# The first tile's queries ahead of the second's, the gate projection by weight blocks, and another split of the same SBUF between two rings

## The reference, cut to what matters

```
u = rmsnorm(h, mix_norm); proj = u @ w_in          # q,k,v of A; z,x,B,C,dt; q,k,v of C
h += concat(y_a, y_b * silu(z) normed, y_c) @ w_out
u = rmsnorm(h, ffn_norm)
q = (u @ w_query).reshape(b, s, 8, 2, 128)         # 8 heads, 2 halves each
sc = einsum("bshtd,htkd->bshtk", q, sub_keys)      # 128 scores in each half
best 16 of 128 per half, best 16 of the 16 x 16 sums -> idx, gates = softmax
act = gelu(u . expert_u[idx]) * gates              # 128 rows of U per token
h += sum(act * expert_v[idx])                      # 128 rows of V per token
h += sigmoid(rmsnorm(h) @ w_gate) * (p @ w_proj)
```

## Time and profile before

| | |
|---|---|
| median of three executions | 3315.85 us (3302.12 to 3317.89) |
| the profiled execution | 3308.7 us, its span 3307.0 us |
| PE, DVE, POOL, ACT busy | 72%, 66%, 59%, 26% |
| bytes moved by DMA | 1267.10 MB, of which 1073.87 MB are gathers |
| granted TensorE clock, mean | 0.834 of full speed |

### The profile page before, as it was taken

The page is one execution under the profiler, slowest core; times in us unless marked ns, Lnnn a source line. Parts: engine busy times, 40 slices in busy tenths (PEclk is TensorE's granted clock), DMA queues, the critical chain, the costliest instruction groups (busy, mean ns, idle before and its releaser), DMA issues.

```text
span 3307.0 us, 34117 instructions
## 1 busy us (share of the span) xinstructions
PE 2395.4 (72%) x11010; PEld 1176.1 (36%) x11010; DVE 2177.6 (66%) x5271; ACT 861.7 (26%) x2201; POOL 1966.3 (59%) x2064
## 2 busy tenths in 40 slices
PE   8999787877788879768668778668765445555546
PEld 4754445532333546333323445333321111111111
DVE  1344878777656788695666777695657777777750
ACT  2441333342132233340222223331211111111100
POOL 0001556566566667676566666676667777777763
PEclk9999888887899887878889887978887767777668
DMA  5426999999999999999999999999999999999996
GB/s 190 144 96 223 374 400 420 362 399 401 420 421 421 414 420 417 413 393 420 421 420 421 416 419 392 417 404 421 421 420 419 419 420 419 419 420 419 420 416 238
DMA packets 332296, 1267.10 MB, mean 383 GB/s; under 512 B 37288, under 2 KB 43600, under 8 KB 313432
## 3 DMA queue, kind: packets, MB, share of 16 engines
q0 software_dynamic: 294912, 1073.87, 80.4%
q1 hardware_dynamic: 37208, 191.04, 14.5%
HBM read 1256.22 MB, written 12.09 MB: 384 GB/s over the span
## 4 chain that ended last, share of the span: by engine, by line
DMA 33%; PE 26%; POOL 15%; DVE 15%; issue 8%; ACT 3%; POOLq 0%; DVEq 0%; SPq 0%; ACTq 0%
DMA v_ring<-peer_v,idx_v 14%; DMA u_ring<-peer_u,idx_u 13%; POOL v_ring L935 7%; DVE u_ring L1733 7%; PE ps L2195 6%; POOL u_ring L921 6%; PE ps L1924 5%; PE ps L2128 3%; PE ps L2117 3%; DMA front<-peer_v,idx_v 3%; PE ps L2043 2%; DMA front<-peer_u,idx_u 2%; PE ps L2011 1%; POOL front L921 1%; POOL front L935 1%
## 5 line engine op out<-in xcount | busy, mean ns | idle before, releaser
L1733 DVE CUSTOM_DVE_ANT_0 u_ring<-u_ring,ps 128x1024 f32<-128x1024 f32 x917 | 1104.2, 1218 | 486.6 <-DMA u_ring<-peer_u,idx_u 479.1
L921 POOL DMA_INDIRECT u_ring<-peer_u,idx_u x917 | 877.7, 957 | 708.0 <-DVE idx_u L1705 304.0
L935 POOL DMA_INDIRECT v_ring<-peer_v,idx_v x920 | 883.6, 960 | 523.5 <-PE ps L2195 280.0
L2195 PE MATMUL ps<-v_ring,spread 128*32 128x512 f32 x3680 | 690.1, 814 | 568.6 <-DMA v_ring<-peer_v,idx_v 470.2
L1924 PE MATMUL ps<-front 128*128 128x512 f32 x1024 | 455.3, 600 | 3.0 <-ACT front L1216 3.0
L2195 PEld LDWEIGHTS ps<-v_ring,spread 128*32 128x32 f32 x3680 | 138.0, 132 | 881.1 <-issue 879.3
L1924 PEld LDWEIGHTS ps<-front 128*128 128x128 f32 x1024 | 193.1, 192 | 257.8 <-issue 257.5
L2195 PE MATMUL ps<-front,spread 128*32 128x512 f32 x416 | 146.3, 959 | 137.3 <-DMA v_ring<-peer_v,idx_v 104.0
L2128 PE MATMUL ps<-front 128*128 128x512 f32 x512 | 229.9, 606 | 0.4 <-DVE front L1630 0.4
L2043 PE MATMUL ps<-front 128*128 128x256 f32 x768 | 184.9, 396 | 0.5 <-DVE a_neg L1488 0.5
L1733 DVE CUSTOM_DVE_ANT_0 front<-front,ps 128x1024 f32<-128x1024 f32 x107 | 129.9, 1220 | 79.7 <-DMA front<-peer_u,idx_u 78.7
(11 more groups left out here) (266 smaller groups left out, 3045.0 us busy)
## 6 DMA issues: line engine op xcount, KB each, us to landing
front<-weight_blocks SPq DMA_DIRECT2D x140, 1024.0 KB, 7.7
v_ring<-peer_v,idx_v POOLq DMA_INDIRECT x920, 13.5
u_ring<-peer_u,idx_u POOLq DMA_INDIRECT x917, 13.6
front<-x SPq DMA_DIRECT2D x14, 512.0 KB, 8.0
front<-c_bias_all SPq DMA_DIRECT2D x32, 192.0 KB, 5.8
front<-keys_turned SPq DMA_DIRECT2D x4, 1024.0 KB, 12.3
front<-ple_w_gate SPq DMA_DIRECT2D x1, 4096.0 KB, 23.6
out<-front SPq DMA_DIRECT2D x7, 512.0 KB, 6.5
```

Source lines behind the costliest of these rows:

```text
L921: nc.gpsimd.indirect_dma_start(row, None, io["peer_u"][0], bass.IndirectOffsetOnAxis(ap=k.idx_u[:, t % 2, j:j + 1], axis=0)).then_inc(here ...
L935: nc.gpsimd.indirect_dma_start(row, None, io["peer_v"][0], bass.IndirectOffsetOnAxis(ap=k.idx_v[:, m % 2, column:column + 1], axis=0)).the ...
L1733: nc.vector.tensor_tensor_reduce(out=row, in0=row, in1=k.un_ps, scale=1.0, scalar=0.0, op0=ALU.mult, op1=ALU.add, accum_out=k.dots[:, t % ...
L2195: last = mm(k.acc_ps[32 * j:32 * j + 32, half * 512:(half + 1) * 512], centres[:, at:at + 32], row[:, half * 512:(half + 1) * 512], start= ...
```

## The change

Four things change together.

1. The ring of weights has RW = 4 places of half a block (512 KB), 2 MB in place of 3 MB; each block is loaded and given back in two parts (SUB = 2). The SBUF that this frees (2048 columns) goes to two more places for V: RV = 11, and MORE_V falls from 4 to 2, so that the grown ring has 13 places as before. V's gathers begin at slot 33 and not 35.
2. `z` becomes `zh`: one step for each block and both tiles, so each block ends with its own step.
3. In group 0 the first tile goes ahead: its turned activations (`n2_t`) stand before the norm of tile 1, and its `q0` product (`p1`) and its scores before those of tile 1. The other units keep their steps for both tiles.
4. The gates of head 1 (`g_norm` 1) move from before slot 0 to slot 1.

```diff
@@ -38,11 +38,12 @@
 GT = 2
 GROUPS = TILES // GT
 NG = GT * P
-RW, UNIT, WCH = 3, 512, 4
-RU, RV, Q = 7, 9, 4
+RW, UNIT, WCH, SUB = 4, 512, 4, 2
+WR = RW * SUB * UNIT
+RU, RV, Q = 7, 11, 4
 STEPS = P // Q
-MORE_U, MORE_V = 4, 4
+MORE_U, MORE_V = 4, 2
 KEPT = 2
 GROW_U, GROW_V = 735, 693
 EDGE = 4
...
-    c, z, o = c_steps(g), [("z", t, u) for u in range(2) for t in tiles_of(g)], o_steps(g)
+    c, o = c_steps(g), o_steps(g)
+    z = [("zh", g, u, half) for u in range(2) for half in range(2)]
...
-        out += turned[0] + o[2:4] + turned[1] + o[4:] + [("n2", 0, 1), ("n2", 1, 1)]
+        out += turned[0] + o[2:4] + turned[1] + o[4:] + [("n2", 0, 1)]
...
-    return out + [("n2_t", t, half) for t in tiles_of(g) for half in range(2)] + [("hold", g * GT)] * (g > 0)
+    if g == 0:
+        return out
+    return out + [("n2_t", t, half) for t in tiles_of(g) for half in range(2)] + [("hold", g * GT)]
+def first_queries():
+    turned, product = ([[(kind, t, half) for half in range(2)] for t in tiles_of(0)] for kind in ("n2_t", "p1"))
+    keyed = [[("q_t", t, 0), ("q_s", t, 0)] for t in tiles_of(0)]
+    return turned[0] + [("n2", 1, 1)] + product[0] + turned[1] + keyed[0] + product[1] + keyed[1]
...
+    if n == 1:
+        out.append(("g_norm", 1))
...
-    return (front_steps(0) + query_steps(0, [0]) + [] + tops[0] + query_steps(0, [1])
-            + [("un", 0)] + tops[1] + [("g_norm", 0), ("g_norm", 1)])
+    return (front_steps(0) + first_queries() + tops[0] + query_steps(0, [1])
+            + [("un", 0)] + tops[1] + [("g_norm", 0)])
...
-                self.block_end.setdefault(step, []).append(g * UNITS + i)
+                for sub in range(SUB):
+                    self.block_end.setdefault(step, []).append((g * UNITS + i) * SUB + sub)
+                    bank = ended_bank(step) if sub == SUB - 1 else None
+                    freed += bank is None
+                    self.given_back.append((bank, freed))
...
-    def load_block(u):
-        if u >= RW:
-            end = next(step for step, blocks in k.block_end.items() if u - RW in blocks)
-            if end in k.half_no:
-                sp.wait_ge(k.w_free, k.half_no[end] + 1)
-            elif end[0] in ("p", "o"):
-                filled((*end[:3], GT - 1))
+    def load_block(n):
+        if n >= RW:
+            bank, freed = k.given_back[n - RW]
+            if bank:
+                filled(bank)
             else:
-                filled(end)
-        sp.dma_start(k.block(u), k.block_src(u)).then_inc(k.w_in[u % RW], 16)
+                sp.wait_ge(k.w_free, freed)
+        sp.dma_start(k.block(n), k.block_src(n)).then_inc(k.w_in[n % RW], 16)
...
+    def products(g, at, half, keys, tiles, gives=True):
+        for sub in range(SUB):
+            w = block(g, at + half, sub)
+            for key, t in zip(keys, tiles):
+                ps, filled = again(key) if half or sub else open_(key)
+                for j in range(SUB):
+                    c = half * WCH + sub * SUB + j
+                    last = mm(ps, k.uT[:, c, cols(t)], w[:, j, :], start=(c == 0), stop=(c == DCH - 1))
+                if half and sub:
+                    last.then_inc(filled, 1)
+            if gives and not (half and sub):
+                last.then_inc(k.w_free, 1)
...
+    def first_query(t, half):
         if half == 0:
-            last.then_inc(k.w_free, 1)
+            for part in range(2):
+                copied(("n2_t", t, part))
...
-    def z(t, u):
-        w = [block(t // GT, U_Z + 2 * u + half) for half in range(2)]
-        ps, filled = open_(("z", t, u))
-        for c in range(DCH):
-            last = mm(ps, k.uT[:, c, cols(t)], w[c // WCH][:, c % WCH, :], start=(c == 0), stop=(c == DCH - 1))
-        last.then_inc(filled, 1)
+    def z_half(g, u, half):
+        products(g, U_Z + 2 * u, half, [("z", t, u) for t in tiles_of(g)], tiles_of(g))
```

More of the change, by code:

```diff
@@ L399, in plan_banks @@
         kind, *at = step
-        vacated = vacated or step == ("n1", 1) or (kind == "p" and at[1] == "q0")
+        vacated = vacated or step == ("n1", 1) or kind == "p1"
         pool = range(4) if n >= 25 else range(6) if vacated else range(8)
-        if kind == "p":
+        if kind == "p1":
+            t, half = at
+            if half == 0:
+                plan.take(("p", 0, "q0", t), pool, 1, 1, hold=True)
+            else:
+                plan.release(("p", 0, "q0", t))
+        elif kind == "p":
             g, unit, half = at
@@ L409, in plan_banks @@
                     plan.release(("p", g, unit, lt))
+        elif kind == "zh":
+            g, u, half = at
+            for t in tiles_of(g):
+                if half == 0:
+                    plan.take(("z", t, u), pool, 1, 1, hold=True)
+            for t in tiles_of(g):
+                if half:
+                    plan.release(("z", t, u))
         elif kind == "o":
@@ L749, in begin @@
         load_block(0)
+        load_block(1)
         sp.dma_start(k.consts[:], io["const_rows"]).then_inc(k.consts_in, 16)
-        load_block(1)
-        load_block(2)
+        for n in range(SUB, RW):
+            load_block(n)
         sp.dma_start(k.head_row, io["c_rel_bias"][0]).then_inc(k.row_in, 16)
@@ L873, in sync_program @@
             store(*at)
-        for u in k.block_end.get(step, ()):
-            if u + RW < GROUPS * UNITS:
-                load_block(u + RW)
+        for n in k.block_end.get(step, ()):
+            if n + RW < GROUPS * UNITS * SUB:
+                load_block(n + RW)
     sp.wait_ge(k.stored, 16 * (TILES + 1))
@@ L1018, in project @@
                 act_fn(k.q[:, lt, :], ps, ACT.Copy).then_inc(copied_, 1)
+    def first_query(t, half):
+        if half:
+            _, ps, copied_ = filled(("p", 0, "q0", t))
+            act_fn(k.q[:, t, :], ps, ACT.Copy).then_inc(copied_, 1)
     def head_roots(g, kind):
@@ L1343, in scalar_program @@
             cs(*at)
-        elif kind == "z":
-            z(*at)
+        elif kind == "zh":
+            g, u, half = at
+            if half:
+                for t in tiles_of(g):
+                    z(t, u)
         elif kind == "y_n":
@@ L2039, in x_project @@
     def x_project(g, c):
-        w = block(g, U_X + c // 2)
         ps, filled = open_(("x", g, c))
-        for j in range(DCH):
-            last = mm(ps[:, 0:NG], w[:, j, c % 2 * P:(c % 2 + 1) * P], k.uT[:, j, :], start=(j == 0), stop=(j == DCH - 1))
+        for sub in range(SUB):
+            w = block(g, U_X + c // 2, sub)
+            for j in range(WCH):
+                at = sub * WCH + j
+                last = mm(ps[:, 0:NG], w[:, j, c % 2 * P:(c % 2 + 1) * P], k.uT[:, at, :], start=(at == 0), stop=(at == DCH - 1))
+            if sub == 0 and c % 2:
+                last.then_inc(k.w_free, 1)
         last.then_inc(filled, 1)
```

127 lines of the change are left out of this document (71 added, 56 removed).

## The result

The changed kernel takes 3313.26 us in the median of 20 runs (3303.24 to 3321.3), the kernel before 3306.18 in 20 (3295.97 to 3317.89). The ratio is 1.0019, with an interval of 1.001 to 1.0028: slower by 3 to 9 us, and outside the range that was forecast. The profiled run took 3318.65 us.

A forecast was written before the change was run, and what follows sets the result against it. PE bounds until 309 us, DVE until 380, then DMA nearly full. Gains 5.5 (start) + 8 (V) + 5 (z) = 18.5, less 2 for overlap, took 3308.7 to 3292.2; with the median's offset 3295, range 3278 to 3312.

The forecast's parts named there:

- Half blocks cost nothing: Weight ring of 2 MB: refills stay hidden, value nothing; up to 15 us of added dips as the other end.
- by that row the cut costs the DMA engines nothing: From 2300 to 3200 us, 512 KB gathers move at 419 GB/s, so cutting weight transfers was taken as free.
- V's two slots bring 8 us: Middle stream: lateness of PE's `values` stops gathers less; dips give back 4, 3 and 1 us.
- my second rival: Middle dips stay because U stops what V no longer stops; only the start gains: 3303, or 3309 to 3310; chance 0.18.
- The start keeps 5.5 us: Group 0's front: DVE starts 11.2 us sooner, but waiting for group 1's norm roots leaves 5.5 us.
- The chain: Steps into the first gather: product at 276.5, DVE at 287.6, gather at 298.0, `q1` at 296.8, roots at 352.7.
- cost nothing to 2 us: Ahead of the first gather: possible price of half blocks at the one tight place, `o`.
- the tight place at `o`: Ahead of the first gather, `o` stands behind 2.5 MB that SP issues at 246 to 248 us; nothing to 2 us.
- moving the gates of head 1: Ahead of slot 0: saves DVE half a microsecond, swallowed by the same wait at the norm; worth nothing.
- z by blocks brings 5 us: `z` in groups 1 to 3: PE's weight wait goes, worth 3.0 us in group 1, 1 each in groups 2 and 3.
- the slower rival: Groups 1 to 3: the weight ring starves PE, dips grow by two thirds (30 us), giving 3333; chance 0.10.
- the sign that the prediction gave for it: Groups 1 to 3: `p` or `o` waiting for weights would show the prediction wrong; no size given.

The follow-up runs named there:

- the cut alone: Kernel before with each 1 MB weight block loaded by two transfers of 128 rows x 4 KB; 1.0032, 1.0016 and 1.0028 to the kernel before.
- whole blocks: Changed kernel with three 1 MB weight places, one transfer each, and nine V slots; 0.9947, 0.9935 and 0.9954 to the kernel before on three slower chips.
- tiles in turn: Changed kernel with the last two half blocks of each product serving tile 0 with both, then tile 1; 1.0015 to the kernel before, 3309.26 us.
- six half places: Changed kernel with six 512 KB weight places (3 MB) and nine V slots; 0.9976 and 0.9996 to the kernel before on two slower chips.
- its second run: The changed kernel unaltered, with eleven V slots, run again on another full-rate chip; 1.0028 to the kernel before.
- the early norm: Changed kernel with 1 MB weight blocks, nine V slots and group 1's first norm moved behind slot 1; 0.9978 to the kernel before, 3299.53 us.

## Why the prediction was wrong, and where it was right

**Half blocks cost nothing: the step that failed first.** The paragraph on half blocks took nothing as their value, and "by that row the cut costs the DMA engines nothing" took the 419 GB/s of gathers of 512 KB as a sign that 4 KB rows are free. That rate was what the gathers had anyway; the weights' old blocks moved faster, as slices of 421 GB/s in the earlier trace rows said and the 419 of the last stretch confirms. The loss could have been read there: 2 in 421 of the 1920 us in which most of the weights flow is 9.1 us. Measured: 9 us by the cut alone, and 13.5 us for half blocks in four places at full rate. The Trainium skill ("DMA: Bandwidth & Descriptors", the section on bandwidth measured) wants at least 1 MiB a transfer; taken as a rate of each transfer it gave 75 us, where 9 were measured. It had the sign right, and its size is far off in a queue that is kept full.

**V's two slots bring 8 us: the step that failed next.** They bring nothing that the runs can tell: 1.0028 with them and 1.0026 without. It is my second rival's mechanism: POOL is in order and U has seven places. With the ring alone changed, 214 us of waits for V came back as 226 us of waits for U (196 and 227 between the kernel before and the changed one). I had asked only, for each dip, which engine was busy; what was missing was how far DVE was ahead of its ring at that moment.

**The start keeps 5.5 us.** The chain was right: whole blocks follow it within 1.3 us at each step, and in the half blocks the order brought the norm 3.0 to 5.0 us forward. What was wrong is "cost nothing to 2 us", taken as nothing, for the half blocks ahead of the first gather: it was 4.8 us at the norm. I moved the chain's steps as if products still took the tiles in turns of 8 records. Half blocks make it turns of 4: tile 0 leads tile 1 by 1.74 us, not 3.47, and PE waits 2.15 us ahead of the turn instead of 0.44 (tiles in turn shows this by undoing it). `q1` begins at 296.37 with whole blocks, 298.88 and 295.09 in two runs with six half places, 303.90 and 301.91 in two of the changed kernel. The difference between six and four places is earlier: with four, PE waits for weights at about 58 us, 0.98 to 2.44 us in each of the eight runs of such kernels, and never with six or with whole ones. SP's timeline in the changed kernel shows what stands there:

```profile
32.57 10.63 SPq L780 DMA_DIRECT2D front<-weight_blocks  x4
43.24 0.76 SPq L808 DMA_DIRECT2D skew<-ext_rows  x1
46.30 11.72 SPq L780 DMA_DIRECT2D front<-weight_blocks  x4
```

The next half blocks are issued behind a transfer of 2 MB (`skew`), and a ring of 2 MB has less in store to bridge it. That the ring's depth matters is shown by six places; that `skew` is what it has to bridge is read from this order alone. The prediction looked for the tight place at `o`, and it was here.

Two smaller terms of the same part: the copies, turns and scores behind 283.4 add up to 288.2 and not 287.6 (the whole blocks' choice began at 287.14). And moving the gates of head 1 was to save DVE a wait of half a microsecond for ACT; instead DVE waits 3.16 us for ACT's `gexp` there (321.98). By the lines that is swallowed too, since DVE still waits for the norm further down.

**The clock** adds what no step had. In the eight runs with four or six half places, the first queries ahead and the 2.15 us wait ahead of the turn, the product behind it took 8.53 to 10.00 us in six and 7.10 or 7.11 in two. With a wait of 0.43 us it was 7.11 in all four of whole blocks with the first queries ahead, and 7.27 in tiles in turn. With the old order, where PE waits 2.4 to 2.5 us, the 32 records took 15.46 to 17.05 us in all seven runs, and never the 13.90 that the prediction halved. In the changed kernel the granted clock was 0.50, the lower level, from 283 to 286 us; in its second run, with 7.11 us, it was 1.00. That the longer wait makes the lower clock likelier fits these rows; it was not isolated. Other low stretches fall in kernels of both kinds: the x step near 85 us took 5.24 us in the changed kernel and 5.90 in one with whole blocks, against 3.72 in the kernel before and with six places.

**z by blocks brings 5 us.** PE's wait of 8.2 us is gone and 680 to 700 is full, as said. With only the gates' move beside it, it measured 0.9992 (0.998 to 1.0003), so 2.6 us, and not told from nothing.

**PE starved in groups 1 to 3** (the slower rival) is not what cost the time at full rate, though the sign that the prediction gave for it did show: `o` waited twice for weights in group 1, 1.7 us in all (1.4 us in the second run). The dips in the middle did not grow as a whole (410 and 411 against 411 GB/s). On the three slower chips the one wait of 4 to 5 us near 411 us is this rival's mechanism, and part of what six places give back there may be its price; no run isolates it.

**The sum, as measured.** The cut of the blocks +9 us, the start +1.8 in the profiled run and -0.2 in the second (inverses at 359.92 and 357.92, against 358.15), V 0, z -2.6: 8 and 6 us. The two ratios give 6 and 9 us. The sums agree in size; which run has the larger one is not explained, since each start is read from one execution. The profiles show the start to the norm only, and that a microsecond there is a microsecond at the end was taken and not tested. The prediction added up 18.5 us of gain: V's 8 of them failed, and the half blocks' 13.5 us of loss were left out. The base was off too: 3295 had half of the 7.2 us in it by which the median of three runs lay above the profiled one, and the median of twenty is 3306.18, 2.5 below it. That moved the forecast towards the result by luck. With whole blocks the start and z together gave 0.9935 to 0.9954 on three chips, where my forecast without V was (5.5 + 5) / 3306, 0.32%. On a chip of full rate whole blocks with the first queries but without the early norm were not run, so what the early norm brings, and why the gain is 0.22% there and 0.5 to 0.65% on the slower chips, stays open.

## What to carry to other kernels

Where DMA is full, a cut of a transfer has a price even if the bytes stay: compare rates of the same queue before and after, not with another queue that has short rows anyway. When a change has several parts, look for the pair of runs on one chip that differ in one part: one such pair gave the price of the half blocks here. A ring's unit also sets how tiles interleave, and so which tile ends first: draw that order before moving a step that waits on it. More places in one ring only help if the in-order issuer isn't stopped by the next ring a moment later; add up all its waits.

## What the hardware showed unexpectedly

- Two transfers with rows of 4 KB for one with rows of 8 KB: the weights' queue took 18 us more of sixteen engines for 191 MB, on both kinds of chip, and full slices fell from 421 to 419 GB/s.
- Transfers of 512 KB on 64 partitions with 8 KB each: 727 us of the queue instead of 504, and the kernel 7.3% slower.
- Three of the chips moved 370 to 400 GB/s in much of a run where others moved 419, and the same kernel took 3504 to 3514 us there instead of 3305 or 3306. The cause is open.
- The same 16 records took 7.1 or up to 10.0 us in runs of one kernel, with the granted clock at its lower level for 3 us in the slower.
